# Order changed at four seams of a two-block transformer stack on one core: low-rank mix, down products around a turn, the attention's last turn, its head norms

## What is computed

```
o = _diff_attention(q, k, v, lam)                    # 8 heads of 128 columns
o = _rmsnorm(o, diff_ln_g) * (1.0 - lam_init)        # the head norms
h_b = o.reshape(bsz, seq, DIFF_V_WIDTH)
g = jax.nn.sigmoid(gates.reshape(...) + gate_b)
m = g[:, :, 0] * (h_a @ w_branch[0]) + g[:, :, 1] * (h_b @ w_branch[1])
return m @ w_out
```

```
p_prev = jnp.pad(p, ((0, 0), (1, 0), (0, 0)))[:, :-1]
p = p + shift_mu * (p_prev - p)
r, k, v, d_w, d_a, d_g = split_cols(p, [...])
w_log = -jax.nn.softplus(-(decay_base + jnp.tanh(d_w) @ decay_up)) - 0.5
a = jax.nn.sigmoid(iclr_base + d_a @ iclr_up)
g = jax.nn.sigmoid(d_g) @ gate_up
```

## Time and profile before

| what | value |
|---|---|
| median of 3 runs | 2375.27 us (2373.42 to 2376.97) |
| the profiled execution | 2375.44 us, of which the span from first to last instruction is 2373.6 us |
| PE busy | 2316.6 us, 98% of the span |
| DVE busy | 1782.6 us, 75% |
| ACT busy | 1191.0 us, 50% |
| chain that ended last | PE 75%, DVE 14%, ACT 4%, DMA 3%, issue 2%, POOL 1% |
| mean granted PE clock | 0.992 |

### The profile page before, as it was taken

One profiled execution on the slowest core, in us unless ns is written; L12 is line 12 of the kernel. 1 busy time (PEld: TensorE's weight loads), 2 busy tenths in 40 slices (PEclk: granted clock), 3 DMA queues, 4 the chain that ended last, 5 costly groups with the idle time before them and its releaser, 6 DMA issues.

```text
span 2373.6 us, 28811 instructions
## 1 busy us (share of the span) xinstructions
PE 2316.6 (98%) x11906; PEld 1911.8 (81%) x11906; DVE 1782.6 (75%) x1849; ACT 1191.0 (50%) x1417; POOL 120.8 (5%) x145
## 2 busy tenths in 40 slices
PE   9999999999999999999999999989999999999998
PEld 8888877888878888778887887778888788777886
DVE  7875867787777756777877976797877777656875
ACT  5553455365455443554553654524455455555453
POOL 0001000000000010000001001102000000110000
PEclk9999999999999999999999999989999999999999
DMA  9566534565555655365564656304466466344563
GB/s 308 177 229 204 182 108 166 189 212 194 197 176 189 229 198 197 125 209 179 188 224 156 218 181 229 113 5 142 160 213 230 160 213 214 124 160 132 171 202 116
DMA packets 281444, 428.17 MB, mean 180 GB/s; under 512 B 11796, under 2 KB 193684, under 8 KB 281185
## 3 DMA queue, kind: packets, MB, share of 16 engines
q1 hardware_dynamic: 273136, 399.51, 49.9%
q0 software_dynamic: 7632, 26.29, 3.5%
q10 hardware_dynamic: 544, 0.52, 0.1%
HBM read 423.41 MB, written 1.05 MB: 179 GB/s over the span
## 4 chain that ended last, share of the span: by engine, by line
PE 75%; DVE 14%; ACT 4%; DMA 3%; issue 2%; POOL 1%; SPq 0%; DVEq 0%; POOLq 0%; ACTq 0%
PE bank L2117 19%; PE bank L2119 18%; PE bank L2118 18%; DVE wl L1213 6%; PE bank L2209 4%; PE bank L2213 4%; PE bank L2212 4%; ACT wh L632 2%; DVE arena L1813 2%; DMA wf<-in_ffn_w_up 1%; PE bank L2164 1%; DMA wf<-in_ffn_w 1%; POOL rstd L472 1%; PE bank L2186 1%; PE bank L2436 1%
## 5 line engine op out<-in xcount | busy, mean ns | idle before, releaser
L2117 PE MATMUL bank<-wh,xTh 128*128 128x512 f32 x1824 | 723.1, 396 | 9.9 <-DVE xTl L1266 4.0
L1213 DVE TENSOR_TENSOR wl<-wf,wh 128x2048 fp32r<-128x2048 f32 x267 | 606.0, 2287 | 166.3 <-ACT wh L632 165.9
L2119 PE MATMUL bank<-wh,xTl 128*128 128x512 f32 x1824 | 710.5, 390 | 0.0
L2118 PE MATMUL bank<-wl,xTh 128*128 128x512 f32 x1824 | 709.1, 389 | 0.0
L632 ACT ACTIVATE wh<-wf 128x2048 fp32r<-128x2048 f32 x267 | 506.6, 1915 | 179.7 <-PE bank L2119 67.2
L2117 PEld LDWEIGHTS bank<-wh,xTh 128*128 128x128 f32 x1824 | 343.1, 188 | 81.4 <-DVE xTl L1266 5.3
L2119 PEld LDWEIGHTS bank<-wh,xTl 128*128 128x128 f32 x1824 | 342.8, 188 | 72.6
L2118 PEld LDWEIGHTS bank<-wl,xTh 128*128 128x128 f32 x1824 | 343.4, 188 | 67.6 <-issue 0.7
L2117 PE MATMUL bank<-wh,hTh 128*128 128x512 f32 x704 | 277.1, 394 | 0.1
L2119 PE MATMUL bank<-wh,hTl 128*128 128x512 f32 x704 | 274.6, 390 | 0.0
L2118 PE MATMUL bank<-wl,hTh 128*128 128x512 f32 x704 | 274.3, 390 | 0.0
(11 more groups left out here) (378 smaller groups left out, 2539.0 us busy)
## 6 DMA issues: line engine op xcount, KB each, us to landing
wf<-in_ffn_w SPq DMA_DIRECT2D x136, 512.0 KB, 6.1
wf<-in_w_in SPq DMA_DIRECT2D x52, 1024.0 KB, 5.9
wf<-in_ffn_w_gate SPq DMA_DIRECT2D x68, 512.0 KB, 5.9
wf<-in_ffn_w_up SPq DMA_DIRECT2D x68, 512.0 KB, 6.9
wf<-in_ffn_w SPq DMA_DIRECT2D x28, 1024.0 KB, 7.1
wf<-in_ffn_w_down SPq DMA_DIRECT2D x28, 1024.0 KB, 7.6
arena<-in_ffn_w SPq DMA_DIRECT2D x38, 512.0 KB, 7.9
arena<-in_ffn_w SPq DMA_DIRECT2D x16, 1024.0 KB, 5.8
```

The costliest lines, as they stand in the source:

```text
L1213: dve.tensor_tensor(wl[s], wf[s], wh[s].bitcast(f32), ALU.subtract).then_inc(SEM[f"lo{s}"], 1)
L2117: pe.matmul(o, lh, rh, start=start, stop=False)
L2118: pe.matmul(o, lh, rl, start=False, stop=False)
L2119: return pe.matmul(o, ll, rh, start=False, stop=stop)
```

## The change

Instructions are neither added nor removed; the same ones stand in another order.

```
@@ ACT, end of a feed-forward
             silu(1, 5)
+            take_hidden(1, 1)
             if after and norm == LN_RMS:
                 new_square_sum(0)
-            take_hidden(1, 1)
@@ ACT, attention
                 if h == 6:
                     take_x(0, (1, 3))
+                if h == 7:
+                    take_x(1, (4, 5))
                 if h:
                     take_output(h - 1)
-            take_x(1, (4, 5))
             prep(3)
@@ DVE, end of a feed-forward
                 after.scaled(0, lambda: gated(1, 5, half).then_inc(SEM["h_ready"], 1))
+                if after.to_rms:
+                    take_hidden(1, 1)
                 after.pre_variance(0)
...
             after.pre_scaled(0)
-            take_hidden(1, 1)
+            if not (after.layer_norm and after.to_rms):
+                take_hidden(1, 1)
@@ DVE, head norms
-            low(0)
-
             dve.wait_ge(SEM["o_sq"], c.next("o_sq", 16))
             dve.tensor_scalar(oss, oss, 1.0 / P, LN_EPS, ALU.mult, ALU.add).then_inc(SEM["head_var"], 1)
-            first_panel = c.so_far("used1")
-            low(1)
-            dve.wait_ge(SEM["head_rstd"], c.next("head_rstd"))
...
+            low(0)
...
-            heads_out(0)
             dve.wait_ge(SEM["gate_on"], c.next("gate_on", 2))
             for b in range(TB):
-                gate_out(0, 0, b, first_panel)
+                gate_out(0, 0, b)
+            dve.wait_ge(SEM["head_rstd"], c.next("head_rstd"))
+            settle(dve.tensor_scalar(orstd, orstd, laminit[:, l, 1:2], None, ALU.mult))
+            dve.wait_ge(SEM["o_out"], c.next("o_out", 8))
+            heads_out(0)
+            low(1)
             take_x(0)
             heads_out(1)
@@ DVE, low-rank mix
+        dve.wait_ge(SEM["gen1"], c.so_far("gen1") + 1)
+        mixed_in(lora_m, lora_p, "prev0_ld").then_inc(SEM["lmix"], 1)
         c.count("gen0")
         unmixed(k_new, mu_k, 0, 1)
         low(0)
-        mixed_in(lora_m, lora_p, "prev0_ld").then_inc(SEM["lmix"], 1)
         low(1)
         settle(mixed_in(k_new, kp, "prev1_ld"))
@@ PE, end of a feed-forward (two_norms is true for the first block's last layer)
+            if two_norms:
+                pe.wait_ge(SEM["ht_ready"], c.next("ht_ready"))
+                down(3, 1, 1, (0,))
                 turn(0, nxt, "x_ready", (4, 7))
-            pe.wait_ge(SEM["ht_ready"], c.next("ht_ready"))
-            down(3, 1, 1, (0, 1), last=True).then_inc(SEM["used3"], 1)
+                down(3, 1, 1, (1,), last=True).then_inc(SEM["used3"], 1)
@@ PE, attention
             turn_weights()
+            turn(1, u_t, None, (4, 5))
             free(0)
             half_panel(0, 0)
             outputs(6)
-            turn(1, u_t, None, (4, 5))
             turn_weights()
```

More of the change, by code:

```diff
@@ L2350, in ffn @@
             down(2, 0, 1, (1,)).then_inc(SEM["used2"], 1)
-            if nxt is not None:
+            if two_norms:
+                pe.wait_ge(SEM["ht_ready"], c.next("ht_ready"))
+                down(3, 1, 1, (0,))
                 turn(0, nxt, "x_ready", (4, 7))
-            pe.wait_ge(SEM["ht_ready"], c.next("ht_ready"))
-            down(3, 1, 1, (0, 1), last=True).then_inc(SEM["used3"], 1)
+                down(3, 1, 1, (1,), last=True).then_inc(SEM["used3"], 1)
+            else:
+                if nxt is not None:
+                    turn(0, nxt, "x_ready", (4, 7))
+                pe.wait_ge(SEM["ht_ready"], c.next("ht_ready"))
+                down(3, 1, 1, (0, 1), last=True).then_inc(SEM["used3"], 1)
         def into_mixer(src):
```

15 lines of the change are left out of this document (8 added, 7 removed).

## The result

The kernel after takes 2378.69 us (median of 20 runs, 2376.28 to 2384.0), the kernel before in the same sessions 2374.31 us (20 runs, 2371.59 to 2377.87). The ratio is 1.0021, with a 95% interval of 1.0015 to 1.0027; it is worked out over all runs and is not the quotient of the two medians, which is 1.0018. The forecast was 2374.1 us, with a range to 2377.5. The time lies above both.

The account below looks back on a forecast made before the run. PE, busy for 98% of the span, was taken as the bound, so only its waits at four seams pay. Sum: 2375.4 - 2.35 (head norms) - 2.2 (double norm) - 0.0 (low-rank) + 3.2 (clock) = 2374.1 us; range 2370.5 to 2377.5.

Parts of the forecast that it names:

- POOL's power is no wait any more: Head norms: the power takes at most 3.2 us from L1655 to L1659, so it is there by 394.8.
- The term of -2.35 us: Head norms with the last turn: PE released 1.17 us earlier a layer, 2.35 us in both layers.
- the wait at the head norms, 2.5 us: Head norms: PE comes 1.96 us earlier, is released 1.17 us earlier, so its wait grows from 1.71 to 2.5 us.
- the clock, +3.2 us: Two head norms and one low-rank product: the clock falls behind two of three new waits, at 1.6 us each.
- the edge "near" 2.2 us: PE's waits: no fall behind 2.19 us, falls behind 2.27 and 2.55, so the edge for a clock fall is near.
- the double norm: Double norm: PE waits 1.2 us in place of 2.55 with no fall behind; 2.2 us kept, mostly the fall's.
- the last turn's 2.0 us: Attention's last turn: comes 2.0 us earlier, but PE waits longer at the head norms; 0.16 us is left.
- the low-rank part's net of nothing: Low-rank mix: PE's turn comes 1.2 us earlier, but `lora_ups` begins at 1487.0 against 1487.01, gaining 0.0 us.
- the new wait for L973: Ahead of `lora_ups`: PE newly waits about 2.7 us for ACT's copy of the turned low-rank columns.
- Rival 3: Low-rank mix: rows land early, in 3.9 us; PE 2.2 us earlier there, 2370.2 us in all; chance 0.09.
- Rival 2: Whole kernel slower, 2377.0 us: key rows land last (+1.35) and the clock falls behind all three waits (+4.8); chance 0.14.
- key rows that land last: Low-rank mix: the key rows' transfer takes its latest landing and puts all off by another 1.35 us.

Follow-up runs that it names:

- heads_alone: Kernel before with only the head norms' new order; 2379.71 us, ratio 1.0011.
- gates_first: Changed kernel with the two gate products directly behind the head norms' variance and `low` behind them; 2375.63 us, ratio 0.9993.
- lora_alone: Kernel before with only the low-rank mix's new order; 2381.4 us, ratio 1.0019.
- double_alone: Kernel before with only the double norm's new order; 2376.71 us, ratio 1.0002.
- two_waits: Kernel before with double-norm and low-rank parts, low-rank copy ahead of key squares, gate products ahead of `low` at head norms, last turn unmoved; 2370.63 us, ratio 0.9979.
- before_busy: Kernel before with 16 idle PE matmuls in each of the waits at the double norm and low-rank turn; 2376.95 us, ratio 1.0009.
- turn_alone: Kernel before with only the attention's last turn moved; 2379.26 us, ratio 1.0017.
- no_heads: Changed kernel with the head norms put back as before, the other three seams changed; 2380.19 us, ratio 1.0011.
- pool_first: Changed kernel with DVE waiting ahead of `low(0)` for a semaphore POOL raises just ahead of its head-norm power; 2381.58 us, ratio 1.0021.

## Why the prediction was wrong

**Failed: "POOL's power is no wait any more: from L1655 to L1659 it took at most 396.66 - 393.46 = 3.2 us".** Measured from L1657 to L1688: 5.24 us, with a power of 4.88 us. The 3.2 us were taken as a bound, but they held for a power that started ahead of a `low`. The change puts the `low` directly behind the variance, so that the power always starts into it. The trace of before did show the effect: the same power on one column takes 0.56 us where it starts into a DVE instruction on one SBUF input (L1288), and 1.53 us where it starts into one on two SBUF inputs (L1295), ending 0.42 us behind that one's end (185.40 and 184.98). Since both powers and both DVE instructions stand in the profile that the forecast was made from, this could have been read. These are the two pairs from the timelines of before:

```profile
183.70 1.28 DVE L1295 SCALAR_TENSOR_TENSOR y<-y,mv,gains 128x1024 f32<-128x1024 f32 x1
183.87 1.53 POOL L472 TENSOR_TENSOR rstd<-ve,mhalf 128x1 f32<-128x1 f32 x1 [159.26 <-DVE ve L1292]
245.78 1.28 DVE L1288 BATCH_NORM_STATS2 stats<-arena 128x6 f32<-128x512 f32 x2
245.96 0.56 POOL L472 TENSOR_TENSOR rstd<-ve,mhalf 128x1 f32<-128x1 f32 x1 [32.23 <-DVE ve L1292]
```

The term of -2.35 us came out at +0.49.

**Mis-sized: the wait at the head norms, 2.5 us.** It is 3.85, by the 1.17 that were not won and about 0.2 that were lost.

**Mis-sized: the clock, +3.2 us.** The mechanism was right, but all three waits fell and not two, and the first fall was 7 us long and not 3.5. Together they are 2.47 + 1.63 + 1.64 = 5.7 us in the profile. The 1.6 us for a short fall was right (1.62 in B and D of heads_alone, 1.3 to 1.9 over all); a long one costs 2.4 to 2.7. Part of a low stretch can lie inside the wait, where it costs nothing: in the kernel after it began at 398.0 and the turn at 399.65.

**Wrong: the edge "near" 2.2 us.** What followed a wait at the seams, over all profiles:

| wait of PE | place | low clock followed |
|---|---|---|
| 1.7 us | last turn, head norms | 0 of 20 |
| 1.6 to 2.2 us | `lora_ups` | 2 of 6 |
| 2.0 us | norms, heads_alone | 2 of 2 |
| 2.3 us | norms, gates_first | 1 of 2 |
| 2.26 us | low-rank turn | 2 of 4 |
| 2.55 us | double norm | 2 of 4 |
| 2.55 us | `lora_ups` | 2 of 2 |
| 3.5 us | norms | 3 of 4 |
| 3.85 to 4.0 us | norms | 6 of 6 |

The first row counts the last turn in before, heads_alone, lora_alone, double_alone, two_waits and before_busy and the head norms in four of them, in both layers. There is no edge in the table but a chance: none in 20 at 1.7 us, and 9 of 10 from 3.5 us on. In between it does not grow steadily with the wait, and length and place change together in these rows. The waits of 1.8 to 2.23 us in stretches that no edit touches (from 100 us on, the recurrence left out) say the same: behind 10 of 15 the clock fell, and behind 2 of the 27 of 1.4 to 1.8 us. The place of the earlier trace rows, which the forecast took as the wait that passes, is one of them: no fall behind 2.19 us in the kernel before, a fall behind 1.93 in the kernel after. The falls that a single profile shows are then draws. The sum took before's two as given and credited the double norm with all of one of them. Over many runs I estimate that gain at 0.64 + half of 1.55 = 1.4 us, and double_alone's interval, which begins at 0.9992, leaves room for 1.9.

**Right:** the last turn's 2.0 us go into the next wait (turn_alone: A -0.06, 0.16 forecast), the double norm (-2.19, with a wait of 1.19 us, though the size is partly luck: the profile of before held a fall there), the low-rank part's net of nothing, with the new wait for L973. In the kernel after the way to that nothing was another. The low-rank rows landed 3.9 us after issue and not 6.2. In 14 profiles this transfer of 1 KB took 3.9 to 6.2 us, seven times 4.6 or less: the 6.2 was the end of a range, taken for the value. Rival 3 had the landing right, and promised 2.2 us for it. Those came in F against the profile of before, and were that profile's fall: against the old order without a fall, 211.75 stands to 212.2. Where the rows did land late, the forecast's account came true: in no_heads, with 6.0 us, F is 214.02 against 214.05 in the profile of before, PE waits 0.99 us at the low-rank turn (1.1 forecast) and 2.54 us ahead of `lora_ups` (2.7 forecast).

**The rivals.** Rival 2 (slower, 2377.0) has the right sign and its cause in part: the clock behind all three waits. Its other cause, key rows that land last, did not come. A blocked power was in no rival, though the trace of before shows one.

## What stays open

The stretch of the recurrence, from its first product at 1502.38 to the first panel matmul behind it at 1630.80, has the same code in all fourteen kernels. Its profiles took from 128.4 us (before, double_alone, pool_first) over 130.9 (heads_alone, lora_alone) to 136.4 (no_heads). Here are the windows of no_heads and, behind them, of the kernel after:

```profile
1570.00:1600.00 30.00, 26.90 (x448) 0.77 0.01 2
1600.00:1640.00 40.00, 38.61 (x328) 0.66 0.32 101
```
```profile
1570.00:1600.00 30.00, 26.84 (x450) 0.77 0.01 2
1600.00:1640.00 40.00, 36.77 (x357) 0.87 0.49 157
```

The clock is low for 24 to 41 us of it, in a pattern that changes from run to run. Between the profiles this is the largest difference, 8 us. One profile of each kernel can't tell whether an edit ahead of it shifts its chances, so how much of the medians of turn_alone and lora_alone comes from there is not settled. The single parts' ratios add up to 1.0049, the whole change has 1.0021: the parts may share the falls at the norms, but the intervals (each about 0.001 either way) are too wide to say more.

## What to carry to other kernels

- Before moving a small POOL instruction, look at what DVE has under way when it will start. A gate product, with one input from PSUM, left the power at 2.91 us; a `low`, with two from SBUF, made it 4.88.
- A wait taken away in front of another one that ends with a different engine isn't won; it joins the next. Two short waits can be cheaper than one long one: the clock stayed up behind 1.69 and 0.51 us, and fell in three of four cases behind 3.5.
- Where the clock falls in a profile of before, do not credit an edit with the whole fall. Look at several profiles of the same wait.

## What the runs showed of the hardware

- POOL's power: one of 128x16 took 2.91 us where no `low` was under way at its start, and 4.88 to 4.96 us when it started into a `low` of 2.29 us, ending 2.76 or 2.77 us behind it; one of 128x1 took 0.56 and 1.53 us in the same way. A `low` that started into a running power kept its 2.29 us.
- At the seams the clock went to 0.50, that is 1.2 GHz, for 3.5 to 3.75 us or for 7 us, and a fall cost 1.3 to 1.9 or 2.4 to 2.7 us. Behind one and the same wait it came in some executions only: behind the 2.55 us at the double norm in two of four, behind the 3.5 us at the norms in one of no_heads's two layers.
- The POOL transfer of 1 KB at the low-rank mix landed 3.9 to 6.2 us after issue, at the same place of fourteen kernels.
